# The opening of a two-layer decoder kernel: loads in another order, sums of squares on TensorE, modulation dots made ahead

## What is computed

```python
c_act = silu(c)                                   # one row of 1024
sh1, sc1, ... = split(c_act @ ada_w[0] + ada_b[0], 9)
h = x * rsqrt(mean(x * x, axis=-1) + 1e-6) * norm_g[0, 0]
h = h * (1 + sc1) + sh1
gate, up = split(h @ ffn_w_in[0, 0], 2)
```

## Time and profile before

| | us |
|---|---|
| median of 3 runs | 2110.14 (2110.12 to 2112.23) |
| profiled execution, its own time | 2109.24 |
| span of its instructions | 2106.9 |
| TensorE busy in the span | 2045.2 |
| end of the first chunk on TensorE | 60.8 |

### The profile page before, as it was taken

One profiled execution on the slowest core, in us unless ns is written; L12 is line 12 of the kernel. 1 busy time (PEld: TensorE's weight loads), 2 busy tenths in 40 slices (PEclk: granted clock), 3 DMA queues, 4 the chain that ended last, 5 costly groups with the idle time before them and its releaser, 6 DMA issues.

```text
span 2106.9 us, 26044 instructions
## 1 busy us (share of the span) xinstructions
PE 2045.2 (97%) x10332; PEld 1744.3 (83%) x10332; DVE 1155.7 (55%) x1653; ACT 603.3 (29%) x717; POOL 46.2 (2%) x55
## 2 busy tenths in 40 slices
PE   4999999999999999999999999999998999999998
PEld 3788888998898889888888988888877798888886
DVE  6677556655455436887444566644458564333322
ACT  2322221423323223222222323322231333222222
POOL 2000000000000000000000000000002000000000
PEclk9999999999999999999999999999999999999999
DMA  8455555433233143667544254544766423233221
GB/s 319 144 195 192 187 190 175 141 120 105 75 109 105 65 155 116 200 229 232 183 166 150 94 159 148 169 148 149 243 206 232 158 80 100 100 100 100 90 95 55
DMA packets 246575, 314.90 MB, mean 149 GB/s; under 512 B 31904, under 2 KB 219552, under 8 KB 244128
## 3 DMA queue, kind: packets, MB, share of 16 engines
q1 hardware_dynamic: 214160, 287.32, 41.4%
q10 hardware_dynamic: 32336, 26.48, 3.8%
HBM read 290.44 MB, written 27.53 MB: 151 GB/s over the span
## 4 chain that ended last, share of the span: by engine, by line
PE 76%; issue 15%; DVE 4%; DMA 3%; ACT 1%; POOL 0%; SPq 0%; ACTq 0%; POOLq 0%; DVEq 0%
PE ps L1779 18%; PE ps L1780 18%; PE ps L1781 18%; PE ps L1806 7%; PE ps L1807 7%; PE ps L1810 7%; DMA y_dram<-s_buf 1%; DVE ada_first L972 1%; DMA y_dram<-acc 1%; PE ps L2058 1%; DMA sq<-y_dram 1%; DMA csil<-in_c 0%; DVE w_lo L962 0%; PE ps L1901 0%; PE ps L2049 0%
## 5 line engine op out<-in xcount | busy, mean ns | idle before, releaser
L557 ACT ACTIVATE w_hi<-w_raw 128x1024 fp32r<-128x1024 f32 x352 | 345.9, 1029 | 353.7 <-PE ps L1781 241.1
L962 DVE TENSOR_TENSOR w_lo<-w_raw,w_hi 128x1024 fp32r<-128x1024 f32 x172 | 210.2, 1222 | 371.8 <-ACT w_hi L557 369.9
L1779 PE MATMUL ps<-g_hi,w_lo 128*128 128x512 f32 (+1 forms) x952 | 345.7, 363 | 0.0
L1781 PE MATMUL ps<-g_hi,w_hi 128*128 128x512 f32 (+1 forms) x952 | 344.9, 362 | 0.0
L1780 PE MATMUL ps<-g_lo,w_hi 128*128 128x512 f32 (+1 forms) x952 | 344.9, 362 | 0.0
L1779 PE MATMUL ps<-h_hi,w_lo 128*128 128x512 f32 x880 | 344.2, 391 | 0.3 <-DVE w_lo L962 0.3
L1781 PE MATMUL ps<-h_hi,w_hi 128*128 128x512 f32 x880 | 342.7, 389 | 0.0
L1780 PE MATMUL ps<-h_lo,w_hi 128*128 128x512 f32 x880 | 342.6, 389 | 0.0
L1806 PE MATMUL ps<-h_hi,w_lo 128*128 128x512 f32 x688 | 269.8, 392 | 2.3 <-DVE w_lo L962 2.0
L1807 PE MATMUL ps<-h_hi,w_hi 128*128 128x512 f32 x688 | 268.6, 390 | 0.0
L1810 PE MATMUL ps<-h_lo,w_hi 128*128 128x512 f32 x688 | 212.3, 390 | 0.0
(11 more groups left out here) (264 smaller groups left out, 2314.1 us busy)
## 6 DMA issues: line engine op xcount, KB each, us to landing
w_raw<-in_ffn_w_in SPq DMA_DIRECT2D x86, 1024.0 KB, 6.6
ada_raw<-in_ada_w SPq DMA_DIRECT2D x128, 512.0 KB, 4.6
w_raw<-in_ffn_w_out SPq DMA_DIRECT2D x32, 1024.0 KB, 6.5
w_raw<-in_ret_w_in SPq DMA_DIRECT2D x24, 1024.0 KB, 5.3
w_raw<-in_ffn_w_out SPq DMA_DIRECT2D x16, 768.0 KB, 4.5
tb<-s_rec SPq DMA_DIRECT2D x6, 1536.0 KB, 6.7
w_raw<-in_ret_w_out SPq DMA_DIRECT2D x8, 1024.0 KB, 5.1
w_raw<-in_s_w_glu SPq DMA_DIRECT2D x8, 1024.0 KB, 6.1
```

The source lines that it names most:

```text
L557: copy = lambda o, i: nc.scalar.activation(o, i, ACT.Copy)
L962: V.tensor_tensor(w_lo[k % 2][:, 0:HALF, :], w_raw[k % 2][:, 0:HALF, :], raw_f32(w_hi[k % 2][:, 0:HALF, :]), ALU.subtract).then_inc(w_lo_h ...
L1779: nc.tensor.matmul(o, wl, xh, start=start, stop=False)
L1781: return nc.tensor.matmul(o, wh, xh, start=False, stop=stop)
```

## The change

SP asks for the conditioning row directly behind `par`, ahead of its two x pairs; then for tile 2 of `ada_first`, where tile 0 was; then for the weights and tiles 3 to 7 as before. ACT asks for tiles 0 and 1 of `ada_first` first, then for x pairs 2 and 3 and the two halves of `w_raw[1]`. DVE no longer adds the squares. TensorE sums the eight tiles of squares itself: 32 matmuls in place of 4, pair by pair as ACT finishes them, accumulated in four columns of a PSUM bank. DVE makes the shifts and scales of tiles 0, 1 and 2 (`FIRST_AHEAD = 3`) and the first `split_first` before it waits for the sums, and two more `split_first` behind `ms`; the loop over the tiles keeps the dots of tiles 3 to 7 and one `split_first`.

```diff
--- before.py
+++ after.py
@@ -454,14 +454,14 @@
 
 
             sp.dma_start(par[:], ins["par"]).then_inc(par_in, 16)
+            sp.dma_start(csil[:], ins["c"].broadcast_to([P, D])).then_inc(c_row_in, 16)
             for pr in range(2):
                 sp.dma_start(x_sb[:, 2 * pr:2 * pr + 2], ins["x_t"][:, 2 * pr:2 * pr + 2]).then_inc(x_in[pr], 16)
-            sp.dma_start(csil[:], ins["c"].broadcast_to([P, D])).then_inc(c_row_in, 16)
-            sp.dma_start(ada_first[:, 0], ins["ada_first"][0]).then_inc(tile_in[0], 16)
+            sp.dma_start(ada_first[:, 2], ins["ada_first"][2]).then_inc(tile_in[2], 16)
             for h in range(2):
                 r = slice(h * HALF, (h + 1) * HALF)
                 sp.dma_start(w_raw[0][:, r], ffn_in[0][:, r, 0:CW]).then_inc(w_first[0][h], 16)
-            for t in range(2, KT):
+            for t in range(3, KT):
                 sp.dma_start(ada_first[:, t], ins["ada_first"][t]).then_inc(tile_in[t], 16)
             sp.dma_start(sm[:, 0:2], ins["s5_a"]).then_inc(params_in, 16)
             sp.dma_start(s5_const[:], ins["s5_const"]).then_inc(params_in, 16)
@@ -914,13 +914,13 @@
             act.sem_inc(silu_done, 1)
             act.sem_inc(silu_g_done, 1)
             act.sem_inc(o_t_done, 1)
+            for t in range(2):
+                act.dma_start(ada_first[:, t], ins["ada_first"][t]).then_inc(tile_in[t], 16)
             for pr in range(2, OUT_PAIRS):
                 act.dma_start(x_sb[:, 2 * pr:2 * pr + 2], ins["x_t"][:, 2 * pr:2 * pr + 2]).then_inc(x_in[pr], 16)
             for h in range(2):
                 r = slice(h * HALF, (h + 1) * HALF)
                 act.dma_start(w_raw[1][:, r], ffn_in[0][:, r, FF:FF + CW]).then_inc(w_first[1][h], 16)
-                if h == 0:
-                    act.dma_start(ada_first[:, 1], ins["ada_first"][1]).then_inc(tile_in[1], 16)
             act.wait_ge(c_row_in, 16)
             nc.scalar.activation(csil[:], csil[:], ACT.Silu).then_inc(csil_done, 1)
             for pr in range(OUT_PAIRS):
@@ -1178,14 +1178,6 @@
                                        in1=raw_f32(h_hi[:, t]), op0=ALU.add, op1=ALU.subtract).then_inc(h_lo_done, 1)
 
             def begin():
-                dve.wait_ge(sq_done, 1)
-                for pr in range(1, OUT_PAIRS):
-                    dve.wait_ge(sq_done, pr + 1)
-                    st.wait()
-                    st(V.tensor_tensor(squares[:, 0:2], squares[:, 0:2], squares[:, 2 * pr:2 * pr + 2], ALU.add))
-                st.wait()
-                st(V.tensor_tensor(acc[:], squares[:, 0], squares[:, 1], ALU.add))
-                st.wait()
                 dve.sem_inc(acc_done, OUT_PAIRS)
                 dve.sem_inc(x_done, OUT_PAIRS)
 
@@ -1209,24 +1201,27 @@
 
                 dve.wait_ge(par_in, 16)
                 dve.wait_ge(csil_done, 1)
-                first_shift(0)
+                st(V.memset(acc[:], 0.0))
+                for t in range(FIRST_AHEAD):
+                    first_shift(t)
+                    first_scale(t)
+                split_first(0, 0)
                 dve.wait_ge(stat_done, 1)
                 V.tensor_scalar(ms[:], ps[:, 4, 0:TT], 1.0 / D, NORM_EPS, ALU.mult, ALU.add).then_inc(ms_done, 1)
-                first_scale(0)
-                st(V.memset(acc[:], 0.0))
-                for k in range(2):
-                    split_first(k, 0)
+                split_first(1, 0)
+                split_first(0, 1)
                 dve.wait_ge(rbc_done, 1)
                 for t in range(KT):
                     if t >= 4:
                         dve.wait_ge(h_lo_done, t - 3)
                     norm_mult(t)
-                    if t + 1 < KT:
+                    ahead = FIRST_AHEAD <= t + 1 < KT
+                    if ahead:
                         first_shift(t + 1)
                     norm_lo(0, t, 0)
-                    if t in (1, 2):
-                        split_first(t - 1, 1)
-                    if t + 1 < KT:
+                    if t == 1:
+                        split_first(1, 1)
+                    if ahead:
                         first_scale(t + 1)
                 dve.sem_inc(mods_done, ADA_FIRST)
 
@@ -1938,7 +1933,13 @@
                 m.then_inc(rbc_done, 1)
 
             def begin():
-                sum_squares(0)
+                for pr in range(OUT_PAIRS):
+                    pe.wait_ge(sq_done, pr + 1)
+                    for r in range(2 * pr, 2 * pr + 2):
+                        for t in range(TT):
+                            m = nc.tensor.matmul(ps[:, 4, t:t + 1], squares[:, r, t * P:(t + 1) * P], ones[:, 0:1],
+                                                 start=r == 0 and t == 0, stop=r == KT - 1 and t == TT - 1)
+                m.then_inc(stat_done, 1)
                 spread_roots(0)
                 pe.wait_ge(w_lo_half, 3)
                 for t in range(KT):
@@ -2318,6 +2319,7 @@
 
 US_DVE = 2
 CSIL_TILE = 5
+FIRST_AHEAD = 3
 
 
 def landed(n, k):
```

## The result

| | before | changed |
|---|---|---|
| median of 20 runs, us | 2109.59 (2107.47 to 2112.23) | 2112.14 (2108.29 to 2114.92) |
| span of the profiled execution | 2106.9 | 2112.6 |
| end of the first chunk on TensorE | 60.8 | 63.1 |

The ratio is 1.0013 (95% interval 1.0008 to 1.0019), that is +2.7 us (1.7 to 4.0): slower, by less than the 0.2% named in the prediction. The two spans differ by 5.7 us, more than the times do: the profiled execution of the changed kernel was the slowest of its 20 (2114.92), and by the end of the first chunk only 2.3 us of the 5.7 have arisen. Behind the chunk the kernels are the same program, and yet the rest took 2049.5 and 2046.6 us in two traces of the changed kernel, and 2046.1 and 2046.5 in two of the one before.

A forecast was written before the change was run, and what follows sets the result against it. TensorE bounds the kernel, but DVE sets the pace from 19.2 to the first chunk's end at 60.8. Sums +5.6 and loop -4.7 make +0.9: 2110.1, or 2111.0 with the median 0.9 above the profiled execution; range 2106.5 to 2114.5.

The forecast's parts named there:

- The loop: DVE's loop over the tiles: turns 0 and 1 at 2.26 and 3.39 us, in all 25.9 against 30.6, giving 4.7 us.
- The sums on TensorE: In front of `ms`: 64 records without a gap, bound by TensorE, ending at 26.7 against 21.1, 5.6 us later.
- The clock: TensorE during the sums: the lower clock level throughout, 0.213 us a record, as small sums do not raise it.
- The landings: Opening loads: landing times counted from bytes moved before each, queues alternating packet by packet at 0.41 MB a us together.
- it lands at about 11.8: x pair 0 in the opening: needs 3.05 MB moved, including some 230 of ACT's 8 KB packets.
- my fixed point: The row's landing at 11.4 in the kernel before, with 2.86 MB counted as moved; other landings were counted from it.
- My bounds: Pair 0's landing: 10.0 if bytes are shared (sums end 24.9), 12.3 with all 256 ACT packets ahead (27.2).
- the signs that I had named for the rivals: Trace signs: records 0.11 apart with `ms` behind the first split; or silu behind 11.8, its row landed long before.
- The clock's rise: Rival, TensorE's sums: clock rises 5.1 us in, sums end at 22.6, DVE's floor decides, 2107.3 to 2108.1; chance 0.17.
- ACT was not held: Rival, ACT held in issuing loads: until 13, sums end at 30.1, +4.3, 2114.4; chance 0.09 for over 3 us.
- Nothing of it shows: Rival, load order has little effect: pair 0 at about 10, sums end at 24.9, -0.9, 2109.2; pair 0 early 0.10.
- The floor of DVE: Earliest `ms` on DVE: its first `split_first`, waiting for weights landing at 21.4 and ACT's 1 us, ends at 23.7.

The follow-up runs named there:

- the repetition: The changed kernel, unchanged, executed once more for its trace: 2110.40 us, sums begun 1.65 us earlier than in its first trace.

## Why the prediction was right, step by step

**The loop** gave what I said: turns 2.27 and 3.39 for 2.26 and 3.39, the loop 25.9. The run without the early dots confirms it from the other side (29.6, where 3.6 more than 25.9 was counted).

**The sums on TensorE** were sized right: 13.78 us in one run without a gap (I had 13.8), bound by TensorE and not by the squares. The sums alone cost 6.1 us in the opening.

**The clock.** The forecast that one-column sums would run at 1.2 GHz held: 0.21 us a record in every trace that did not start them from the upper level. It rested on the fall at the kernel's end, one case of a mixed stretch, and was given 0.17 to fail. The Trainium skill, "TensorE: Matmul & The Clock Gate", Part 1 (What's actually happening), ties the clock to how busy TensorE was. By that rule 13.78 us of unbroken work should have raised it, and it did not; here the measurement decides. The run with extra matmuls in front shows the clock even falling under such sums.

**The landings** were the term that was mis-sized, in the step "it lands at about 11.8". Packets did alternate, 79 to 80, but pair 0 was squared at 13.20, the row came at 9.43 and not by 8. The rate was not the error: by 11.35 the loads had moved 3.23 MB before and 3.19 after. The count of bytes ahead of the pair was. At its landing 3.92 MB had moved where I had counted 3.05, and at the row's landing before, my fixed point, 3.23 where I had counted 2.86. So my count was short by 0.9 MB for the pair and by 0.4 at the fixed point, and the difference of 0.5 MB is 1.2 us at 0.41 MB a us. In the repetition 3.35 MB had moved: short by 0.3, and the estimate fits. Which packets went ahead in one execution and not in the other, these views do not show. All loads from 0 to 13.15 in this trace, and from 0 to 11.5 in the repetition:

```profile
DMA packets 883, 3.92 MB, mean 298 GB/s; under 512 B 80, under 2 KB 208, under 8 KB 627
...
DMA packets 736, 3.35 MB, mean 291 GB/s; under 512 B 67, under 2 KB 195, under 8 KB 486
```

The repetition, with 11.54, shows that the estimate lay at the early edge of a spread with its mean at 12.5. My bounds (10.0 to 12.3) took in how the queues share, not that the first loads vary, and this trace lies outside them. With the mean, the sum is +0.9 + 0.7 = +1.6; with this trace's, +0.9 + 1.4 = +2.3, which is what its last `norm_mult` shows.

**The size.** +0.9 was forecast and +2.7 (1.7 to 4.0) measured, inside the range and within 0.2%. That says little by itself: the range of 8 us also held the times of all three rivals (2107.3 to 2108.1, 2114.4 and 2109.2), and the forecast was a small difference of two larger terms, +5.6 and -4.7. What speaks for the mechanism is that the trace shows each of them, +7.1 (the sums end at 28.17 and not at 21.12) and -4.7, and none of the signs that I had named for the rivals. 0.7 of the difference in time is the landings. Some 1.1 us stays open; the interval reaches nearly down to the +1.6, and the time behind the first chunk differed by 3 us between two traces of the changed kernel (2049.5 and 2046.6), so the runs here can't say whether it is real.

**The rivals.** The clock's rise did not happen. ACT was not held: its table load was at 4.97 and silu waited for its row. "Nothing of it shows" needed pair 0 at about 10. The floor of DVE, 23.7 in my count, was at 25.0, behind tile 2 and the weights that also landed later; the run with the x pairs ahead shows it deciding, at 26.0.

## What to carry to other kernels

- Work moved to an idle engine is free only if it ends before its result is wanted. Here four adds on DVE, which let the sums start 3.0 us behind the last square (16.26 to 19.28), became 56 more one-column records (12 us) in front of `ms`, and that alone made `ms` 6.1 us later. Letting DVE make all or a part of the adds in its waits took 1.8 to 3 us back.
- Loads with large rows on one queue slowed loads with small rows on the other, packet for packet (79 to 80 packets, 0.52 to 0.32 MB): put first on both queues what is wanted first, count the bytes ahead of it on both, and give the landing a margin for its spread, here 1.7 us.
- When dots or other work leave a loop, look at what they had covered. Here two turns then waited 0.85 us each for ACT, and one dot in each turn took that back.

## What the runs showed of the hardware

TensorE, busy 2.96 of 3.00 us with one-column sums at 2.4 GHz, was put down to 1.2 GHz at 18.6, and in the next execution at 17.0, so that 16 such records took 1.90 us at first and 3.57 later. At the lower level, 64 of them without a gap (13.78 us) did not raise it. And the opening loads of one order began the sums at 14.39 in one execution and at 12.74 in another, while with the old order three executions agreed to 0.13 us.
